# A ring of six gathered expert rows in place of eight, in a streaming encoder layer with a product-key expert stage

## The reference, cut to what matters

```
q = (xb @ w_pq).reshape(t, PEER_HEADS, 2, PEER_HALF)
s = einsum('thpd,phkd->thpk', q, keys)
top_s, top_i = top_k(s, 16)
cand_s = top_s[:, :, 0, :, None] + top_s[:, :, 1, None, :]
best_s, best_j = top_k(cand_s, 16)
g = softmax(best_s)
h = einsum('td,thkd->thk', xb, u_emb[expert])
act = g * gelu(h)
out = einsum('thk,thkd->td', act, v_emb[expert])
```

## Time and profile before

| | us |
|---|---|
| median of 3 runs | 3471.99 |
| lowest and highest of the 3 | 3468.22, 3472.59 |
| profiled execution, span | 3471.7 |
| first gather issued | 658.93 |
| last dot product begins | 3455.24 |

### The profile page before, as it was taken

How to read it: one execution, slowest core, us unless ns; L and a number is a source line. 1 busy time by engine, 2 the same in 40 slices (tenths; PEclk the granted TensorE clock), 3 DMA queues, 4 the chain that set the end, 5 groups by cost and what they waited for, 6 DMA issues and landing times. The chain is left out here.

```text
span 3471.7 us, 41167 instructions
## 1 busy us (share of the span) xinstructions
PE 2483.2 (72%) x13379; PEld 1018.3 (29%) x13379; DVE 2488.9 (72%) x6867; ACT 996.6 (29%) x2816; POOL 1454.8 (42%) x1266
## 2 busy tenths in 40 slices
PE   7999889676667666766766676667666766766764
PEld 4444666422222222222222222222222222222221
DVE  4888678677677767776776777777777766767885
ACT  3333444322232222222222222222222222222331
POOL 2333231144444444444444444444444444535443
PEclk9999889798888888888888888878888888888877
DMA  4000200799999999999999999999999999999997
GB/s 154 27 24 21 75 31 19 276 421 421 420 412 419 420 413 418 415 416 417 416 415 416 411 412 418 419 413 416 417 419 414 413 419 416 402 366 421 413 421 328
DMA packets 194557, 1198.43 MB, mean 345 GB/s; under 512 B 31051, under 2 KB 41379, under 8 KB 55102
## 3 DMA queue, kind: packets, MB, share of 16 engines
q0 software_dynamic: 156672, 1140.92, 79.8%
q1 hardware_dynamic: 37694, 55.13, 4.6%
HBM read 1181.14 MB, written 14.84 MB: 344 GB/s over the span
## 5 line engine op out<-in xcount | busy, mean ns | idle before, releaser
L1311 PE MATMUL ps<-uv_rows,diag 64*64 64x512 f32 x8704 | 1355.1, 748 | 898.7 <-ACT diag L1433 896.9
L1220 POOL DMA_INDIRECT uv_rows<-in_uv_emb,experts x1088 | 1287.0, 1183 | 1510.2 <-PE ps L1311 1304.2
L1582 DVE CUSTOM_DVE_ANT_0 uv_rows<-uv_rows,xn_c 128x1024 f32<-128x1024 f32 x1088 | 1332.7, 1225 | 740.1 <-DMA uv_rows<-in_uv_emb,experts 734.7
L1311 PEld LDWEIGHTS ps<-uv_rows,diag 64*64 64x64 f32 x8704 | 325.4, 154 | 1638.8 <-ACT diag L1433 1206.7
L1425 ACT ACTIVATE gelu_c<-dots 128x2 f32<-128x2 f32 x544 | 110.7, 204 | 1754.1 <-DVE dots L1582 1753.9
L1433 ACT ACTIVATE diag<-ident_twice,act_c 128x64 f32<-128x64 f32 x1088 | 319.2, 340 | 286.6 <-DVE act_c L1599 285.9
L1274 PE MATMUL ps<-w_pq_sb,xnT_c 128*128 128x256 f32 x1152 | 350.5, 435 | 1.2 <-ACT xnT_c L1395 1.2
L1274 PEld LDWEIGHTS ps<-w_pq_sb,xnT_c 128*128 128x128 f32 x1152 | 223.0, 211 | 270.5 <-issue 246.8
L577 DVE SCALAR_TENSOR_TENSOR convT<-w_out_sb,tapsT,convT 128x128 f32 (+1 forms) x960 | 252.8, 343 | 0.0
L517 PE MATMUL ps<-w_in_sb,w_out_sb 128*128 128x512 f32 (+1 forms) x656 | 241.7, 524 | 12.2 <-ACT w_out_sb L403 12.2
L339 POOL TENSOR_TENSOR rstd_a<-ms_a,neg_half 128x1 f32<-128x1 f32 x9 | 85.6, 9509 | 181.1 <-ACT ms_a L384 181.1
(11 more groups left out here) (208 smaller groups left out, 2100.9 us busy)
## 6 DMA issues: line engine op xcount, KB each, us to landing
uv_rows<-in_uv_emb,experts POOLq DMA_INDIRECT x1088, 12.6
w_in_sb<-in_w_in SPq DMA_DIRECT2D x4, 2048.0 KB, 11.7
w_pq_sb<-in_w_pq SPq DMA_DIRECT2D x8, 1024.0 KB, 12.0
cat_turned<-catT SPq DMA_DIRECT2D x9, 512.0 KB, 2.6
w_out_sb<-in_x_prompt SPq DMA_DIRECT2D x8, 512.0 KB, 3.6
w_out_sb<-in_w_out SPq DMA_DIRECT2D x1, 4096.0 KB, 16.0
catT_c<-cat_turned SPq DMA_DIRECT2D x8, 512.0 KB, 8.0
out<-x_c SPq DMA_DIRECT2D x8, 512.0 KB, 8.2
```

Of the source, the lines that this page charges most:

```text
L1220: nc.gpsimd.indirect_dma_start(out=rows[:, m % RING, :], out_offset=None, in_=d.uv_emb[0], in_offset=bass.IndirectOffsetOnAxis(ap=experts[ ...
L1311: ins = pe.matmul(ps[dst, 2 * x + half, :], diag[src, (m + i) % DIAGS, :], rows[src, (m + i) % RING, cols], start=first, stop=last)
L1582: nc.vector.tensor_tensor_reduce(out=row, in0=row, in1=xn[:, block_of(n) % 2, :], scale=1.0, scalar=0.0, op0=ALU.mult, op1=ALU.add, accum_ ...
```

## The change

The ring has six slots. The tile in SBUF keeps its size of eight rows, 64 KB on each partition; the last two are no longer written by gathers. The key matrices stay where they were, in the eighth row.

```diff
-        RING = 8
+        RING = 6
+        SPARE = 2
-        rows = sb("uv_rows", [P, RING, 2 * s.D])
-        keys = rows[:, RING - 1, :].rearrange("p (x e) -> p x e", e=s.HALF)
+        rows = sb("uv_rows", [P, RING + SPARE, 2 * s.D])
+        keys = rows[:, RING + SPARE - 1, :].rearrange("p (x e) -> p x e", e=s.HALF)
```

## The result

With six rows the kernel takes 3755.2 us (median of 4 runs, 3743.3 to 3764.0) against 3471.4 us for the kernel before. The ratio is 1.0817, with a 95% interval from 1.0793 to 1.0841. The forecast was 3600 us with a range up to 3790. The direction was right and the time lay within the range, but the loss is 284 us where the sum had 125.

A forecast was written before the change was run, and what follows sets the result against it. The prediction took the 16 DMA engines to bound the expert stage. To 3471.7 us it added 45 for head starts and 80 for engine lags: 3597, taken as 3600, range 3478 to 3790.

The forecast's parts named there:

- L without queue: Expert stage: a gather's time from issue to landing with no others queued ahead, estimated at 5.7 us.
- Start, tail and the move of the keys' wait: Ring's first gathers, the stretch behind the last dot, and the transposed-keys wait moved to gather 5: 0 us each.
- The time from landing to release: From the landing of a pair's even row to the next issue into its slot: about 7.9 us.
- The sign: Whole kernel: the chance that the change makes it slower, 0.82.
- Ordinary laps: Slot laps outside head starts: a 13.6 us loop against DMA's 14.9 us, hidden by 1.3 us.
- Head starts: Laps through a head's first pair, with ACT's table loads: 0.7 us over for each of 68 heads, 45 us.
- Lags of single engines: One DMA engine falling behind leaves others dry: one further share of 80 us, the least certain term.
- The drain's 3.4 us: End of the gathers: the last landing came 3.4 us after evenly shared transfers would end, read as the slowest engine's lag.
- Rival A: Expert stage: landing stays 9.1 us, so the 17.0 us loop binds every lap; 290 us more, 3760; chance 0.28.
- The page's rule: A GpSimd-issued DMA takes 2.0 us plus bytes over 436 GB/s: 4.4 us per gather, loop 12.3 us, time 3472.
- Case B: The shorter ring is hidden, as gathers always find the DMA engines busy: 3472 us; chance 0.14.
- The clock: TensorE's granted clock: PEclk should stay within a few hundredths of 0.86.

The follow-up runs named there:

- the run with half the columns: Six rows, with the matmuls of the second 512 columns of the v rows left out, against the kernel before: 3562 us, ratio 1.0269.

## Why the prediction was right and wrong

**Right.** DMA bounds the kernel before, and there is a loop of landing and release whose queue is the cover: eight rows with a shorter release gain nothing, seven lose nothing. The DMA share fell to 0.97, where 0.96 was named. L without queue was taken as 5.7 us; the shortest measured is 5.5 us, and the median with nothing ahead, in the four-row kernel, 5.8 us. Start, tail and the move of the keys' wait cost nothing. The time from landing to release stayed about what it was (8.2 us from even dot to issue before, 8.4 us after). The two things that the prediction named as proof against it, an L far from 5.7 us and a changed release, did not come, and still the loss is more than twice its sum: the fault lies in how it used them. The sign was given 0.82.

**The step that failed: "Ordinary laps. 5.7 + 7.9 = 13.6 us against 14.9: hidden, by 1.3 us."** This compared the sum of a *shortest* landing and a *mean* release with the time that a saturated engine needs. It put the ordinary laps at nothing, and they are where most of the loss lies: the intervals that were to stay at 2.49 us inside a head are longer in every row, and the row behind a head's first pair has 71 of the 275 us. In the traces, 90% of the pairs are issued 3.2 to 7.7 us after the pair before them with eight rows (median 4.9), and 3.2 to 8.9 us with six (median 5.4). With little cover a pair that comes late costs the engines time (the 219 pairs over 6 us apart, whose dots follow at 6.0 us), and one that comes early queues, which gives nothing back. So an even row takes 8.5 us from issue to dot in the mean, not 5.7, while the engines move 9% less than they can (379 against 416 GB/s), and the lap is 8.5 + 8.4 = 16.9 us in place of 14.9. The right question was not whether the mean loop fits but by how much it must, given its spread. With the measured parts, seven rows have 3.8 us of cover and are enough; the 1.1 us of six rows are not, and the 2.2 us of the run with half the columns still lose 92 us.

**Head starts, 45 us.** They are late, if less than the three examples of the earlier trace rows suggested: from even dot to issue 9.4 us in the mean of all heads, where all pairs have 8.4 and the examples had 9.9. The row that they let go loses 71 us, so the term was too small. Its cause was named wrongly in part: without the table loads the head starts are as late as with them. What does make them late stays open; their matmuls take 3.2 us in the mean, those of the other pairs 2.6 us.

**Lags of single engines, 80 us.** The drain's 3.4 us was read as something the kernel needs cover for. Seven rows show that it isn't: the last engine's lag shrinks from 4.3 to 1.8 us, free of charge. What scattered delays cost with six rows was not shown, so no run says what should stand in the place of the 80 us.

**Rival A** named 3760 us and hit the time, by luck. Its mechanism, a landing that stays at 9.1 us whatever the queue, is not what happened: landings of 5.5 us exist, five rows had 7.8 us and not 9. It was near because at six rows the mean landing *with* its uneven queue happens to be 9.1 us. It also gave seven rows rightly as free.

**The page's rule** of 2.0 us plus bytes over 436 GB/s (the Trainium skill, "DMA: Bandwidth & Descriptors", section "Anatomy of one DMA — SWDGE (gpsimd) path") gives 4.4 us for this gather. The shortest landings are 5.3 to 5.5 us from the start of POOL's instruction, which itself lasts 0.95 us; without it 4.4 to 4.6 us are left. So the trace agrees with the rule for the shortest landings; the median gather with nothing ahead of it, 5.8 us, leaves 4.8 us. Case B, built on it, failed for the same reason as the forecast.

**The clock** fell from 0.862 to 0.835, inside what the prediction allowed, and is a small part of the loss (some 30 us, the estimate above).

## What to carry to other kernels

A ring of buffers ahead of a saturated DMA path has to cover the mean loop plus its spread. In this kernel, whenever the sum of best landing and mean release came within one transfer of the lap (1.1, 2.2 and 2.4 us of cover against 2.49), time was lost, and with 3.8 us none. Measure one size more and one less: here the eighth row was free to give up, and the seventh was worth 8%. Seven rows leave 8 KB of every partition at no cost.

How soon the next transfer is let go matters as much as how many there are. At most four rows under way with 2.0 us from dot to issue ran at 3515 us, a ring of six with 8.4 us at 3755 us. (The first still holds eight slots of memory, so it is no kernel to copy.)

Judge a DMA path by GB/s against its best stretch. Its busy share stood at 0.97 while 9% of the rate was gone.

## What the runs showed of the hardware

- Rows that start late show as longer packets, not only as gaps: in a gather with nothing ahead of it the first packets took 0.6 to 1.35 us where others take 0.31 us. Over the whole run the same bytes cost 152 us more packet time, and the median packet was the same.
- To follow the row ahead at the full rate (2.5 us), a gather had to be issued over 4 us before that row had its eighth increment; with 1 to 2 us of lead it followed at 3.7 us.
- This gather of 1.05 MB ran at the full rate with 4.0 rows, 4 MB, in flight. 3.2 rows gave 91% in pairs with 1.1 us of cover and 99% singly with 2.4 us; 2.4 rows gave 79 to 82%.
- A one-run DMA issued by POOL from memory to memory fell on the same one of the 16 engines, by the increments and the time: 268 of them cost an otherwise full path 419 us, 1.6 us each.
- Matmuls of 64 rows by 64 columns in different quarters of the array overlap fully here: leaving out two of the four quarters saved nothing (1442.7 against 1447.7 us).
